# Two query blocks' attention scores at a time, in two places of each head's loop

## The reference

```python
def blk(args):                      # one block of 128 query rows
    qi, i = args
    qpos = i * Q_BLOCK + jnp.arange(Q_BLOCK)
    s = jnp.einsum('bqhcd,bkhcd->bhcqk', qi, k).astype(F32) * scale     # c: the two maps
    s = jnp.where(kpos[None, :] <= qpos[:, None], s, -jnp.inf)
    p = diff_probs(s, lam)          # softmax of map 0 - lam * softmax of map 1
    return jnp.einsum('bhqk,bkhv->bqhv', p.astype(v.dtype), v)
```

## Time and profile before

| | |
|---|---|
| median of 3 runs | 2231.82 us |
| the profiled execution | 2233.89 us, span of its instructions 2232.1 us |
| granted TensorE clock over the span | 0.999 of 2.4 GHz |
| busy share | TensorE 99%, weight loads 95%, DVE 68%, ACT 54%, POOL 44% |
| heads stage | about 64 to 1032 us of the span |

### The profile page before, as it was taken

The page is one execution under the profiler, slowest core; times in us unless marked ns, Lnnn a source line. Parts: engine busy times, 40 slices in busy tenths (PEclk is TensorE's granted clock), DMA queues, the critical chain, the costliest instruction groups (busy, mean ns, idle before and its releaser), DMA issues. The chain is left out here.

```text
span 2232.1 us, 48427 instructions
## 1 busy us (share of the span) xinstructions
PE 2204.0 (99%) x19103; PEld 2118.4 (95%) x19103; DVE 1517.7 (68%) x2529; ACT 1204.8 (54%) x2499; POOL 988.5 (44%) x1186
## 2 busy tenths in 40 slices
PE   7999999999999999999999999999999999999999
PEld 6899999999999999999898999999999999999999
DVE  5767677776767676775767425318988888876534
ACT  6667676767767676766443421125566666644110
POOL 1147272745555472727322124441256565635431
PEclk9999999999999999999999999999999999999999
DMA  8222222122222222222789523112354555485212
GB/s 311 67 65 81 67 88 67 59 87 76 80 71 85 74 72 68 88 67 97 299 307 363 212 51 124 38 57 94 122 185 174 188 185 191 172 313 193 86 48 96
DMA packets 103515, 288.37 MB, mean 129 GB/s; under 512 B 18426, under 2 KB 26490, under 8 KB 103290
## 3 DMA queue, kind: packets, MB, share of 16 engines
q1 hardware_dynamic: 102138, 281.09, 35.6%
q10 hardware_dynamic: 1152, 4.19, 0.5%
HBM read 213.18 MB, written 63.77 MB: 124 GB/s over the span
## 5 line engine op out<-in xcount | busy, mean ns | idle before, releaser
L173 PE MATMUL ps<-xn_hi,h_w_hi 128*128 128x344 f32 x1680 | 550.1, 327 | 2.3 <-PEq L206 0.9
L173 PE MATMUL ps<-xn_lo,h_w_hi 128*128 128x344 f32 x1680 | 536.6, 319 | 0.0
L173 PE MATMUL ps<-xn_hi,h_w_lo 128*128 128x344 f32 x1680 | 536.5, 319 | 0.0
L173 PEld LDWEIGHTS ps<-xn_hi,h_w_hi 128*128 128x128 f32 x1680 | 317.1, 189 | 20.7 <-issue 12.8
L173 PEld LDWEIGHTS ps<-xn_lo,h_w_hi 128*128 128x128 f32 x1680 | 315.8, 188 | 0.6
L173 PEld LDWEIGHTS ps<-xn_hi,h_w_lo 128*128 128x128 f32 x1680 | 315.8, 188 | 0.0
L1314 POOL TENSOR_TENSOR h_w_lo<-h_w_raw,h_w_hi 128x1024 fp32r<-128x1024 f32 x58 | 139.9, 2413 | 356.7 <-DVE h_a_E L1528 192.2
L3279 DVE SCALAR_TENSOR_TENSOR x<-ps,keep_mod,x 128x344 f32<-128x344 f32 x168 | 94.1, 570 | 162.6 <-PE ps L3116 99.7
L3116 PE MATMUL ps<-f_act_lo,f_d_hi 128*128 128x344 f32 x528 | 169.4, 321 | 0.0
L3116 PE MATMUL ps<-f_act_hi,f_d_lo 128*128 128x344 f32 x528 | 168.8, 320 | 0.0
L3116 PE MATMUL ps<-f_act_hi,f_d_hi 128*128 128x344 f32 x528 | 168.4, 319 | 0.2 <-DVE x L3279 0.2
(11 more groups left out here) (494 smaller groups left out, 6706.9 us busy)
## 6 DMA issues: line engine op xcount, KB each, us to landing
h_w_raw<-in_w_in SPq DMA_DIRECT2D x72, 512.0 KB, 3.5
y_rows<-f_y SPq DMA_DIRECT2D x44, 516.0 KB, 2.6
f_y_pair<-y_rows SPq DMA_DIRECT2D x22, 1032.0 KB, 5.3
h_d_ada_w<-in_w_ada SPq DMA_DIRECT2D x32, 512.0 KB, 3.8
g_vp<-in_cache_v SPq DMA_DIRECT2D x32, 512.0 KB, 6.0
f_a<-in_w_ffn SPq DMA_DIRECT2D x57, 256.0 KB, 2.6
g_kp<-in_cache_k SPq DMA_DIRECT2D x28, 512.0 KB, 7.8
h_w_raw<-in_w_mix SPq DMA_DIRECT2D x24, 512.0 KB, 3.5
```

The lines of the kernel that those rows point to most:

```text
L173: ins = eng.matmul(out, w[:, k * P:(k + 1) * P], x[:, k, columns], start=(k == 0 and n == 0), stop=(k == n_k - 1 and n == 2))
```

## The change

Only TensorE's order moves. The scores of block 1 go from ahead of the eight transposes of the values to behind them, right ahead of block 2's. The scores of block 3 go from ahead of dense piece 2 to behind it, and block 4's, which stood ahead of dense piece 3, follow at once. Block 4's scores overwrite block 2's, so a wait for block 2's exponentials stands between them (`exped.at(h, 2)`).

```diff
             for h in range(H):
                 pe.wait_ge(qk_ready.sem, qk_ready.at(h, 0))
-                scores_of(h, 0)
                 pe.wait_ge(piece_read.sem, piece_read.at(h, 0))
                 if h:
                     pe.wait_ge(o_rstd.sem, o_rstd.at(h - 1, 2))
                 turn8(Xf, vT).then_inc(v_turned.sem, 1)
+                scores_of(h, 0)
                 pe.wait_ge(o_read.sem, o_read.at(h, 0))
                 pe.wait_ge(st_ready.sem, st_ready.at(h, 0))
+                scores_of(h, 1)
...
                 for i in range(NB):
-                    if i + 1 < NB // 2:
-                        scores_of(h, i + 1)
                     for n in ATT_PIECES[i]:
                         if n == ATT_PIECES[i][0] and i >= 2:
                             pe.wait_ge(pv_read.sem, pv_read.at(h, i - 1))
                         piece(h, n)
+                    if i == 1:
+                        scores_of(h, 2)
+                        pe.wait_ge(exped.sem, exped.at(h, 2))
+                        scores_of(h, 3)
                     if 0 < i:
                         values(i - 1, ATT_PIECES[i][-1])
```

## The result

The changed kernel takes 2238.80 us (median of 9 runs, 2237.62 to 2240.54) where the kernel before takes 2233.42 us beside it (9 runs, 2231.39 to 2234.32): ratio 1.0028, interval 1.0019 to 1.0037. By the ratio it is slower by 6.2 us (4.2 to 8.3 by the interval; the medians alone differ by 5.4), a little over the 0.2% that can be told from no change. The profiled execution took 2238.59 us, its span 2236.8.

The account below looks back on a forecast made before the run. TensorE, busy 99%, bounds the kernel, but VectorE sets block 4's transposes in seven of eight heads. 7 x 0.85 - 0.6 = +5.35 us gave 2237.2 us against the 2231.82 median; range 2230.0 to 2239.0.

Parts of the forecast that it names:

- the size of the loss in a head: Block 4's transposes in heads 1 to 7 come later by +0.85 us per head, bounds 0.5 to 1.0.
- the start of GpSimd's low part: GpSimd's operation on the low part of a weight tile, after block 2's weighing, starts at 216.25 instead of 215.40, +0.85.
- the squeeze of GpSimd's list: VectorE's weighing of block 2 falls among GpSimd's squares; taking turns at SBUF adds about 0.3 us.
- POOL's list alone: Lower bound for the low part's start: 215.9, +0.5, if only GpSimd's own seven operations, shifted by 0.88, delay it.
- GpSimd's old 0.43 us of waiting: Before the change GpSimd, its seven operations done at 214.96, waits 0.43 us for block 2 before the low part.
- It keeps TensorE's -0.6: Head 0 has no earlier head's squares and no wait at block 4, so it gains TensorE's full 0.6 us.
- the one entry and exit saved at the scores of blocks 3 and 4: Both blocks' 64-row scores, set behind one another, pay the price of going in and out once: -0.4 us per head.
- the head's start: From the recurrence's matmuls to the first dense piece, one time in and out goes: -0.2 us, bounds 0 and -0.3.
- block 3's tiny maxima operation: VectorE's two-column last operation of block 3's maxima ends with GpSimd's low part, at 218.65 instead of 217.80.
- The clock rival: TensorE's clock falls in the new 1.5 us wait; in half of the heads +6 on top, 2243; chance 0.08.
- The rival that TensorE's saving comes through: VectorE finishes block 4 by 227.1, so all eight heads gain 0.6: -4.8, 2227.0 us; chance 0.12.
- The even case: Low part stays in place as GpSimd squeezes its list; only head 0 gains 0.6: 2231.2 us; chance 0.20.

Follow-up runs that it names:

- the first part alone: Kernel before with only block 1's scores moved behind the eight transposes, blocks 3 and 4 left as they were: 2238.85 us, ratio 1.0027.
- the extra square: Kernel before with GpSimd's first square of each head done twice, TensorE's order untouched: 2242.22 us, ratio 1.0041.
- the single square that was added or taken away: GpSimd's first square per head done twice in the kernel before (2242.22 us), or left out of the changed kernel (2234.89 us).
- the kernel before with the norms late: Kernel before with both pairs of VectorE's gate norms moved behind weighing block 4, ahead of block 5's maxima: 2243.38 us, ratio 1.0043.
- the change with the sums ahead: Changed kernel with TensorE's first sum ahead of both score sets, ScalarE's root earlier, VectorE's second norms in idle time: 2231.76 us, ratio 1.0000.
- the first four experiments: Only block 1's scores moved (2238.85 us); only blocks 3 and 4's (2235.84); a square added to the kernel before (2242.22); one left out of the change (2234.89).
- the two kernels with the norms in idle time: Changed kernel and kernel before, each with both norm pairs moved behind block 5's maxima, into VectorE's idle time: 2232.32 and 2233.18 us.

## Why the prediction was wrong, and what of it held

**The step that failed** is the size of the loss in a head, +0.85 us, and in it the start of GpSimd's low part. The prediction put that start between +0.5 and +1.0 and took +0.85; it measured +1.04, past the upper bound. What went into it was nearly right: block 1's delay was 0.87 (0.88 forecast), GpSimd's start 0.86, and the squeeze of GpSimd's list 0.29 (5.52 us from the first square's start to the last copy's end, 5.23 before; 0.3 forecast). The sum of the two was wrong. "215.9 (POOL's list alone, +0.5)" has the low part start 0.06 behind the end of the list at 215.84, so that nearly all of GpSimd's old 0.43 us of waiting is there to absorb delay. But in the change, where the low part has nothing but GpSimd's own list to wait for, 0.33 us lie between the two, in all seven heads; and 0.33 again in the first part alone and with the extra square. So the old wait absorbed 0.10, and the shift was 0.86 + 0.29 - 0.10 = 1.05. A head took 1.01 more, not 0.85; 1.1 us over seven heads. What GpSimd does in those 0.33 us stays open.

**A second term failed with it: head 0.** "It keeps TensorE's -0.6" came to nothing: from block 1's transposes to block 4's, head 0 takes 15.76 us, 15.74 before. In head 0 no sums stand behind the weighted values, and without the scores there nothing covers ScalarE's read; TensorE and ScalarE in head 0 of the change:

```profile
92.53 0.38 PE L1244 MATMUL ps<-keep_ident,h_a_E 128*128 128x128 f32 x2
93.06 0.42 PE L173 MATMUL ps<-xn_hi,h_w_hi 128*128 128x344 f32 x1
```

```profile
92.73 0.28 ACT L1002 ACTIVATE h_d_oraw<-ps 128x128 f32<-128x128 f32 x1 [1.38 <-PE ps L1219]
```

TensorE's own entries were sized better: the one entry and exit saved at the scores of blocks 3 and 4 gave 0.36 (0.4 forecast), the head's start 0.12 (0.2 forecast).

**The sum.** In place of 7 x 0.85 - 0.6 = 5.35 the heads lost 7 x 1.01 = 7.0. The two profiles have 6.2, because 0.9 is missing behind the heads, for which the prediction has no term and no run shows a cause in the change. That the measured 6.2 us (2238.80 against a forecast of 2237.2) still came out near the forecast is in part luck: errors of 1.1 and 0.6 on one side, and 0.9 on the other.

**What held** is the place, the chain and the sign: the loss is at block 4's transposes in seven heads, by way of block 1's scores, GpSimd's list, block 3's tiny maxima operation and VectorE's weighing. The first part alone, and the single square that was added or taken away, moved it by themselves; that is shown, not only argued. The clock rival is out: from 100 to 1000 us of the changed kernel's span the granted clock is 1.00, so no head lost clock in its new wait.

**The rival that TensorE's saving comes through** was priced with one holder, the low part. There were more behind it: the norm's wait for its sum (0.47 a head by itself), and ScalarE's exponentials and reads. Even with the first two moved away, 0.16 of 0.6 came through. Its chance of 0.12 was not too low. The even case had 0.20 for a reason that turned out void, since GpSimd's own wait absorbed only 0.1.

## What to carry to other kernels

Where an engine is 99% busy, ask of each operation that is moved later not whether that engine minds, but which queue starts on its result: here the effect came 22 us later, by way of an engine 44% busy. A delay can be followed through four engines to 0.2 us in the timeline, but an idle time in the row is not all there to absorb it: of 0.43 us here only 0.10 was. The gain has to be followed in the same way: each of the holders removed here uncovered another one. And an operation that looks wasteful between two others (scores between transposes and a dense piece) may be what covers a read; count what it covers before moving it.

## What was not expected of the hardware

The stretch at the lower clock ahead of head 0 belongs to single executions, not to an order of TensorE's work. The same two windows in the profile of the change, then in that of the kernel before with the norms late, whose head 0 is that of the kernel before:

```profile
79.20:80.80 1.60, 0.35 (x3) 0.06 (x1) 1.60 (x4) 0.46 (x1) 0.00 (x0) 1.00 0.00 0
81.60:84.95 3.35, 3.35 (x30) 3.05 (x29) 2.17 (x8) 1.43 (x6) 0.00 (x0) 1.00 0.96 328
```

```profile
79.20:80.80 1.60, 0.43 (x6) 0.44 (x6) 1.06 (x3) 0.50 (x2) 0.00 (x0) 1.00 0.00 0
81.60:84.95 3.35, 3.35 (x26) 3.04 (x24) 2.30 (x10) 1.73 (x5) 0.32 (x3) 1.00 1.01 349
```

Both stay at 2.4 GHz (granted clock 1.00), while the profile of the change with the sums ahead has a mean of 0.55 in the second window, though its head 0 begins with the eight transposes as well. Of the 14 profiles of this study 6 have the stretch (a mean clock of 0.86 from 78 to 90 us) and 8 have 1.00 there, with either order in both groups. The six reach block 1's transposes of head 0 on average 1.3 us later (87.83 and 86.56 us). This accounts for most of the 1.46 us by which the profiled execution of the change was ahead at head 1, and for part of the spread of 2 to 3 us between executions of one kernel: the granted clock over the whole span is 0.999 in those six and 1.000 in the eight, and on the chip of the first four experiments the kernel before takes 2231.71 us in the mean of 13 executions at 1.000 and 2233.25 in the mean of 12 at 0.999. Sorted like this, the two kernels with the norms in idle time, changed order and old, take 2231.66 and 2232.87 (8 executions each at 1.000), 1.2 us apart, as seven times 0.16 has it. What decides the clock from one execution to the next stays open.
